# Blocks 0 and 1 by seven products too, and weights split into high and low parts in every unit

## The chip, the cores and the metric

One Trainium2 chip, one of its cores. The metric is the device time of one execution in microseconds (us). TensorE (PE) multiplies, VectorE (DVE), ScalarE (ACT) and GpSimd (POOL) do the rest, and SyncE (SP) issues the transfers between the chip's memory (HBM) and the on-chip SBUF. Each engine works through its own list in order; semaphores join the lists.

## The reference, cut to what matters

```
hn   = rms_norm(x, norm_g)                          # x: 4096 + 32 rows of 1024
proj = hn @ w_in                                    # 1024 x 3584
h, b, c, z, a, g, zb = split(proj)                  # seven sections of 512
out_a  = b * causal_conv3(c * h) * silu(z)
conv_b = causal_conv31(a * sigmoid(g)) + conv_b_bias
out_b  = silu(layer_norm(conv_b)) * silu(zb)
y = rms_norm(x + concat(out_a, out_b) @ w_out, final_norm_g)
```

The histories of the two convolutions are outputs too.

## The kernel before, in words

The tokens are 9 blocks of 460 (12 of padding). Every float32 product is made of three matmuls: each operand is split into a high part and a low part (operand minus high part), and `split_product` adds high x high (L1737), high x low (L1738) and low x high (L1739). A matmul of 128 x 128 weights on 460 tokens is the unit of work here.

The first projection runs in **5 units**: unit 0 has blocks 0 and 1, units 1 to 3 two blocks each, unit 4 block 8. A unit has **14 periods**, in the order of `ORDER` (ga0 zz0 hc0 ga1 bz0 hc1 bz1 ga2 zz1 hc2 ga3 bz2 hc3 bz3), each for 128 columns of each of two sections: ga makes v (for conv31), hc makes u = c h (for conv3), bz the gate of group A, zz the two silu gates. Period n is 14 x unit + position, 0 to 69; periods 13, 27 and 41 are the last of units 0, 1 and 2.

- **Unit 0** has four `standing_tile`s a period, 24 matmuls each, 96 in all. The weights of the period come as float32 and are split there: high parts on ScalarE (`weight_high`, L1132), low parts on VectorE (`weights_low`, L1396, 128x1024 twice), the four sums of weights that the products of later units need on GpSimd (`weight_sums`, L929 to L934, and their low parts, L940). All eight finished chunks, high and low, go to HBM (`weight_forms`).
- **Units 1 to 3** multiply by the method of Strassen: seven products of 12 matmuls, 84 a period, in the order P1, P5, P6, P2, P7, P3, P4 (`strassen_product`). P3 waits for ScalarE's copy of P5, P6 for that of P1, P7 for that of P6, P4 for that of P7 (`copy`, L1172). P1 starts when the last tile of two periods ago is read. Each product reads a finished chunk of weights from a ring of 9 slots (`load_form`), and a *form* of x: a sum or difference of quarters of the unit's scaled x, split into high and low. The seven forms of the next unit are made around its start: sums on VectorE (`form_sum`, L1405 to L1417), high parts on ScalarE (`form_high`, L1150), low parts on VectorE (`form_low`, L1424).
- **Unit 4** multiplies plainly: two tiles of two half tiles of 12 matmuls a period (`late_tile`), each with a finished chunk of the ring.

Beside these: VectorE makes the 620 taps of conv31 (L1554), a number for each period (`tap_quota`: 10 in an inner period of units 0 to 3, 12 in unit 4); in `finish(n-1)`, run in period n, it multiplies the first block of a section (L1479 for u) and runs conv3 (`conv_a`, L1503, L1506). In units 1 to 3 `first_tile_sums` (L1439, L1442) adds products for the first block, GpSimd adds the last quarter (`last_quarter`, L1002) and makes the second block of v, u and the gate (`second_block`, L976, L980, L984), and ScalarE applies the gates in place (`gate_in_place`, L1183). GpSimd also scales x (`x_scale`, L905). In unit 4 the layer norm of group B begins: GpSimd's `sums` (L1012, L1015) and `sum_low` (L1020) wait for conv_b to come back from HBM, TensorE makes the mean and the variance (`channel_mean`, L1844), and the out projection's weights are split (`out_weight_low`, L1032). After unit 4 come layer norm, out projection and the last norm for all tokens; the change doesn't touch that part.

The order on each engine is written out by hand, as one loop over the periods for each; the taps are placed by `tap_plan`. `sets` are the four quarters of the two last periods, `ps` is PSUM, `w_ring` the ring, `xf` the forms of x, `x_raw` the scaled x.

## Time and profile before

| what | value |
|---|---|
| median of 3 runs | 1589.77 us (1589.3 to 1589.8) |
| the profiled execution | 1589.94 us, its span 1588.1 us |
| instructions: TensorE / VectorE / ScalarE / GpSimd | 7196 / 1196 / 721 / 434 |
| first matmul on x | 24.03 us |
| HBM read / written | 277.70 MB / 101.18 MB |

Span is from the first to the last instruction on record. The trace gives for every instruction its start, its length and, in brackets, how long its engine stood idle before it and what it waited for. Matmul records overlap, so their number in a stretch tells more than their lengths. The matmul lengths on record are those of a pipeline and aren't to be multiplied by a count; the time from one to the next is.

### The profile page before, as it was taken

Reading aid. Unit: us, or ns where it says so; the run is one execution under the profiler, and the core shown is the slowest. Engines: PE = TensorE matmul, PEld = TensorE weight load, DVE = VectorE, ACT = ScalarE, POOL = GpSimd, SP = SyncE. Lnnn points to the kernel's source line nnn. Section 1 sums busy time; section 2 is a strip of 40 time slices with the busy share of each in tenths; the row PEclk is TensorE's granted clock in tenths of the full one; section 3 lists DMA queues with packets and bytes.
Section 4 is the critical chain, followed back from the end, with each engine's and each line's share of the span. In section 5 each row is a group of like instructions: output and inputs, shape, how many; then the busy total and the mean of one; then the engine's idle time right before and its main releaser. Section 6 shows DMA issues by size and latency. Waiting matters only on the chain.

```text
span 1588.1 us, 19038 instructions
## 1 busy us (share of the span) xinstructions
PE 1544.5 (97%) x7196; PEld 1356.8 (85%) x7196; DVE 1281.0 (81%) x1196; ACT 509.0 (32%) x721; POOL 501.1 (32%) x434
## 2 busy tenths in 40 slices
PE   4899999999999999999999999999999999999998
PEld 4789999988888888888888888888887888888886
DVE  5699899997877998879798878785997777777752
ACT  4443433333333243332253312232231232323221
POOL 3756869201232221132221131113220333332310
PEclk9999999999999999999999999999999999999999
DMA  4898889689987788897779877779576443545441
GB/s 157 321 332 311 324 305 353 241 296 304 283 285 241 232 254 295 277 290 252 234 222 310 259 231 243 220 256 318 192 241 198 138 145 142 184 160 182 142 142 63
DMA packets 105613, 380.06 MB, mean 239 GB/s; under 512 B 16228, under 2 KB 20196, under 8 KB 101944
## 3 DMA queue, kind: packets, MB, share of 16 engines
q1 hardware_dynamic: 105528, 378.93, 71.4%
q8 instruction: 54, 0.88, 0.2%
q14 instruction: 31, 0.25, 0.0%
HBM read 277.70 MB, written 101.18 MB: 239 GB/s over the span
## 4 chain that ended last, share of the span: by engine, by line
PE 90%; DVE 6%; issue 2%; DMA 1%; POOL 1%; ACT 0%; POOLq 0%; DVEq 0%; SPq 0%; ACTq 0%
PE ps L1737 30%; PE ps L1739 30%; PE ps L1738 30%; DVE ps L1554 3%; DVE xf L1396 1%; DVE xf L1388 1%; DVE x_raw L1382 1%; DMA conv_b<-conv_spill 1%; DMA w_ring<-weight_forms 0%; PE ps L1844 0%; DVE w_ring L1396 0%; PE ps L1845 0%; POOL ln_tmp_a_f L1012 0%; POOL w_out_split L1032 0%; DVE conv_b L1571 0%
## 5 line engine op out<-in xcount | busy, mean ns | idle before, releaser
L1554 DVE SCALAR_TENSOR_TENSOR ps<-v,conv_b_taps,ps 128x920 f32<-128x920 f32 (+2 forms) x580 | 630.9, 1088 | 18.0
L1737 PE MATMUL ps<-xf,w_ring 128*128 128x460 f32 x1624 | 605.2, 373 | 3.3 <-DMA w_ring<-weight_forms 2.1
L1739 PE MATMUL ps<-xf,w_ring 128*128 128x460 f32 x1624 | 604.1, 372 | 0.0
L1738 PE MATMUL ps<-xf,w_ring 128*128 128x460 f32 x1624 | 602.7, 371 | 0.0
L1737 PEld LDWEIGHTS ps<-xf,w_ring 128*128 128x128 f32 x1624 | 306.4, 189 | 39.0 <-issue 3.3
L1738 PEld LDWEIGHTS ps<-xf,w_ring 128*128 128x128 f32 x1624 | 306.4, 189 | 34.7
L1739 PEld LDWEIGHTS ps<-xf,w_ring 128*128 128x128 f32 x1624 | 305.9, 188 | 35.1
L1172 ACT ACTIVATE sets<-ps 128x460 f32<-128x460 f32 x168 | 92.8, 552 | 460.3 <-PE ps L1739 456.5
L1737 PE MATMUL ps<-w_out_split,mixed 128*128 128x512 f32 x528 | 206.5, 391 | 0.0
L1739 PE MATMUL ps<-w_out_split,mixed 128*128 128x512 f32 x528 | 206.4, 391 | 0.0
L1738 PE MATMUL ps<-w_out_split,mixed 128*128 128x512 f32 x528 | 206.3, 391 | 0.0
L1002 POOL TENSOR_TENSOR sets<-sets 128x460 f32<-128x460 f32 x42 | 55.0, 1310 | 425.1 <-ACT sets L1172 425.1
L1737 PEld LDWEIGHTS ps<-w_out_split,mixed 128*128 128x128 f32 x528 | 99.5, 189 | 21.8 <-issue 1.0
L1739 PEld LDWEIGHTS ps<-w_out_split,mixed 128*128 128x128 f32 x528 | 99.5, 188 | 20.9
L1738 PEld LDWEIGHTS ps<-w_out_split,mixed 128*128 128x128 f32 x528 | 99.4, 188 | 20.8
L1342 ACT ACTIVATE ps<-h_rows 128x1024 f32<-128x1024 f32 (+1 forms) x33 | 34.0, 1029 | 213.6 <-DVE h_rows L1685 213.6
L879 POOL TENSOR_TENSOR row_mean_sq_eps<-row_mean_sq,rms_eps 128x1 f32<-128x1 f32 (+1 forms) x33 | 9.0, 274 | 282.2 <-ACT ps L1342 282.2
L1737 PE MATMUL ps<-xf 128*128 128x460 f32 x224 | 84.7, 378 | 10.8 <-DVE xf L1388 10.8
L1739 PE MATMUL ps<-xf 128*128 128x460 f32 x224 | 84.3, 376 | 0.0
L1738 PE MATMUL ps<-xf 128*128 128x460 f32 x224 | 83.6, 373 | 0.0
L905 POOL TENSOR_TENSOR x_raw<-x_raw,rstd_spread 128x460 f32<-128x460 f32 x56 | 69.4, 1272 | 44.9 <-DMA rstd_spread<-rstd_spill 44.9
L1685 DVE TENSOR_TENSOR h_rows<-ps,x_rows_again 128x1024 f32<-128x1024 f32 (+1 forms) x33 | 40.2, 1218 | 39.3 <-PE ps L1739 39.3
(144 smaller groups left out, 1575.0 us busy)
## 6 DMA issues: line engine op xcount, KB each, us to landing
w_ring<-weight_forms SPq DMA_DIRECT2D x350, 512.0 KB, 5.1
weight_forms<-xf SPq DMA_DIRECT2D x14, 2048.0 KB, 11.2
weight_forms<-w_ring SPq DMA_DIRECT2D x14, 2048.0 KB, 13.5
x_raw<-in_xT SPq DMA_DIRECT2D x18, 920.0 KB, 11.4
x_rows_again<-in_x_prompt SPq DMA_DIRECT2D x32, 512.0 KB, 4.3
out_y_prompt<-h_rows SPq DMA_DIRECT2D x32, 512.0 KB, 3.0
xf_f<-in_w_in SPq DMA_DIRECT2D x26, 512.0 KB, 6.3
x_row<-in_x_prompt SPq DMA_DIRECT2D x28, 460.0 KB
```

Of the source, the lines that this page charges most:

```text
L905: pool.tensor_tensor(part, part, spread[:, 0:TB], ALU.mult).then_inc(x_scaled, 1)
L1002: pool.tensor_tensor(sets[:, s, QC, :], sets[:, s, QC, :], sets[:, s, QD, :], ALU.add).then_inc(c22_made, 1)
L1172: act.activation(sets[:, n % 2, quarter, :], ps[:, bank, 0:TB], ACT.Copy).then_inc(copied, 1)
L1342: act.activation(out_pair(2)[0:rows, :], hrow[0:rows, s, :], ACT.Square, scale=RMS_SCALE, accum_out=ssq[0:rows, s:s + 1]).then_inc(h_sumsq, 1)
L1382: dve.scalar_tensor_tensor(part, part, gain[:, k:k + 1], ps[:, FIRST_BANK[b], 0:TB], ALU.mult, ALU.mult).then_inc(x01_scaled, 1)
L1388: dve.tensor_tensor(standing_x(b, 1, 2 * r, 2 * r + 2), st[:, 2 * b + r // 2, 2 * (r % 2):2 * (r % 2) + 2, :], standing_x(b, 0, 2 * r, 2 * ...
L1396: dve.tensor_tensor(chunks(g, 2 * f, 2 * f + 2)[:, :, 1, :], raw_weights(g, f), chunks(g, 2 * f, 2 * f + 2)[:, :, 0, :].bitcast(F32), ALU. ...
L1554: dve.scalar_tensor_tensor(dst, window, wb[:, j, k:k + 1], part, ALU.mult, ALU.add).then_inc(taps_done, 1)
L1685: dve.tensor_tensor(hrow[0:rows, s, :], out_pair(s)[0:rows, :], raw[0:rows, s, :], ALU.add).then_inc(h_done, 1)
L1737: pe.matmul(out, ahi, bhi, start=(start and x == 0), stop=False, skip_group_check=goes_on)
L1738: pe.matmul(out, ahi, blo, start=False, stop=False, skip_group_check=goes_on)
L1739: mm = pe.matmul(out, alo, bhi, start=False, stop=(stop and x == len(terms) - 1), skip_group_check=goes_on)
```

## The change

- Unit 0 goes through the seven products too. Its `standing_tile` is gone, and `first_tile_sums`, `last_quarter` and `second_block` run there as in units 1 to 3. Periods 0 and 1 are interleaved (`FIRST_PRODUCTS`), and seven forms of x are made at the start from halves (`first_sum_of_x`, `first_form_high`, `first_form_low`).
- The order of products is P1, P5, P6, **P3**, P7, **P2**, P4.
- Only the four sums of weights are stored (`weight_sums`, 2 MB a period for 4 MB). The weights as they stand are read again as float32 (`load_chunk`, 256 KB for the 512 KB of a finished chunk) and split again: in units 1 to 3 three chunks a period, high on ScalarE (`ring_high`), low on GpSimd (`ring_low`); in unit 4 all 56 (`late_high`, `late_low`), 128x512 each.
- In unit 0 ScalarE, VectorE and GpSimd handle chunks of 128x512 one at a time: three low parts of weights on VectorE, four sums and four low parts on GpSimd.
- At a unit's start the forms of P3 and P2 change places, and P4's form gets a place of its own.
- Taps per inner period are 9, 10, 11, 11 and 12 in units 0 to 4. The first layer norm's steps on VectorE move from positions 8, 10 and 12 to 9, 11 and 13, and the variance from 8 to 9.

```diff
-CHUNK_OF = [0, 4, 5, 1, 6, 7, 3]
-P1, P5, P6, P2, P7, P3, P4 = range(7)
+P1, P5, P6, P3, P7, P2, P4 = range(7)
+
+WEIGHT_OF = {P1: 0, P2: 1, P4: 3}
+SUM_OF = {P5: 0, P6: 1, P3: 2, P7: 3}
+S1, S2, S4, S3 = range(4)
+SUM_ORDER = [S1, S2, S4, S3]
+PRODUCT_OF_SUM = [P5, P6, P3, P7]
+PRODUCT_OF_WEIGHT = [P1, P2, P4]
...
+FIRST_PRODUCTS = [(0, P1), (1, P1), (0, P2), (1, P2), (0, P5), (0, P3), (0, P6), (0, P7), (0, P4),
+                  (1, P5), (1, P6), (1, P3), (1, P7), (1, P4)]
...
-    return 10 if u < 4 else 12
+    return [9, 10, 11, 11, 12][u]
...
-        forms_d = nc.dram_tensor("weight_forms", [G14, P, 8 * 2 * HC], F32).ap()
+        forms_d = nc.dram_tensor("weight_sums", [G14, P, 4 * 2 * HC], F32).ap()
...
+                if i in WEIGHT_OF:
+                    load_chunk(g, WEIGHT_OF[i], slot)
+                else:
+                    src = forms_d[g].rearrange("p (c l m) -> p c l m", c=4, l=2)
+                    sp.dma_start(ring[:, slot, :, :].bitcast(F32), src[:, SUM_OF[i]]).then_inc(ring_in[slot], 16)
...
-                load_ring(r // 4, r % 4, late_slot(r))
+                load_chunk(r // 4, r % 4, late_slot(r))
...
+            def sums_of_weights(g):
+                for x in SUM_ORDER:
+                    weight_sum(g, x)
+                for x in SUM_ORDER:
+                    sum_low_half(g, x)
+
+            def ring_low(n, i):
+                pool.wait_ge(ring_hi, weights_split(n, i))
+                w = weights(n, i)
+                pool.tensor_tensor(w[:, 1, :], weights(n, i, True)[:, 1, :], w[:, 0, :].bitcast(F32),
+                                   ALU.subtract).then_inc(ring_lo, 1)
...
+            def rings_low(n):
+                if n >= G14:
+                    ring_low(n, P2)
+                    ring_low(n, P4)
+                if G14 <= n + 1 < III:
+                    ring_low(n + 1, P1)
...
+            for n in range(1, III):
+                last_quarter(n - 1)
                 edges(n - 1)
-                if n + 1 < II:
-                    weight_sums(n + 1)
-                    sums_low(n + 1)
-                carry(n - 1)
+                if n < G14 - 1:
+                    second_block(n - 1)
+                    carry(n - 1)
+                    sums_of_weights(n + 1)
+                else:
+                    rings_low(n)
+                    second_block(n - 1)
+                    carry(n - 1)
...
 
             for n in range(III, PERIODS):
                 g = n - III
                 if n == III:
                     last_quarter(n - 1)
                 edges(n - 1)
+                late_low(4 * g + 2)
+                late_low(4 * g + 3)
                 second_block(n - 1)
                 carry(n - 1)
+                if 1 <= g <= KC:
+                    out_weight_low(g - 1)
+                late_low(4 * g + 4)
+                late_low(4 * g + 5)
                 if g == 3:
                     sums(0, 0)
                     sum_low(0)
...
+                    wait_a_free(act, n)
+                    copy(n, P1, QA, copied_a)
                 if ends and w < 4:
                     form_high(w, P1)
                 elif ends:
                     x8_high(0)
                     x8_high(1)
+                rings_high(n)
                 gate_in_place(n - 1)
-                if begins:
-                    form_high(unit(n), P3)
                 wait_d_free(act, n)
                 copy(n, P5, QD, copied_d)
+                if begins:
+                    form_high(unit(n), P4)
                 if ends and w == 4:
                     x8_high(2)
                     x8_high(3)
...
-            first_ln = {5: centre, 6: square_sums, 7: var_low, 8: normalise, 10: gate, 12: b_low}
+            first_ln = {5: centre, 6: square_sums, 7: var_low, 9: normalise, 11: gate, 13: b_low}
...
+
+            for n in range(1, III):
                 w, g = unit(n) + 1, n % G14
+                if n == 1:
+                    weight_low(1, P4)
+                elif n < G14:
+                    weight_low(n, P2)
+                    weight_low(n, P4)
                 if g == 0:
-                    form_low(unit(n), P2)
-                if n > II:
-                    first_tile_sums(n - 1)
+                    form_low(unit(n), P3)
+                first_tile_sums(n - 1)
                 if g == 0:
+                    form_sum(unit(n), 3)
                     finish(n - 1)
                     form_low(unit(n), P7)
-                    form_sum(unit(n), 3)
-                    form_low(unit(n), P3)
+                    form_low(unit(n), P2)
                     form_low(unit(n), P4)
...
-            for n, t in TILE_AT:
-                standing_tile(n, t)
-                if (n, t) == (0, 1):
+            for n, i in FIRST_PRODUCTS:
+                strassen_product(n, i)
+                if (n, i) == (0, P1):
                     first_statistics(1)
-                if (n, t) == (1, 0):
                     first_rstd(1)
```

**ScalarE, the last period of unit 1 (period 27).** From the copy of P1 on; `sets<-ps` are copies of products, `xf<-` the high parts of the next unit's forms. Before:

```order
L1172 ACTIVATE sets<-ps 128x460 [waits product_done,spilled_ab_1]
L1150 ACTIVATE xf<-x_raw 128x920 [waits x_scaled,product_done]
L1150 ACTIVATE xf<-x_raw 128x920
L1172 ACTIVATE sets<-ps 128x460 [waits product_done,spilled_dc_1,last_quarter_summed]
L1172 ACTIVATE sets<-ps 128x460 [waits product_done,spilled_ab_1]
L1150 ACTIVATE xf<-xf_f 128x920 [waits x_form_sums,product_done]
L1150 ACTIVATE xf<-xf_f 128x920
```

After (L1250 copies, L1224 makes high parts):

```order
L1250 ACTIVATE sets<-ps 128x460 [waits product_done,spilled_ab_1]
L1224 ACTIVATE xf<-x_raw 128x920 [waits x_scaled,product_done]
L1224 ACTIVATE xf<-x_raw 128x920
L1188 ACTIVATE w_ring<-w_ring_f 128x512 [waits w_ring_in_1]
L1188 ACTIVATE w_ring<-w_ring_f 128x512 [waits w_ring_in_2]
L1188 ACTIVATE w_ring<-w_ring_f 128x512 [waits w_ring_in_3]
L1250 ACTIVATE sets<-ps 128x460 [waits product_done,spilled_dc_1,last_quarter_summed]
L1250 ACTIVATE sets<-ps 128x460 [waits product_done,spilled_ab_1]
L1224 ACTIVATE xf<-xf_f 128x920 [waits x_form_sums,product_done]
```

Three high parts of weights, each behind its load, have moved in between the first form of x and the copy of P5.

**GpSimd, periods 27 and 28.** `u<-sets` is u's second block, `conv_a_acc<-` the gate's second block, `sets<-sets` a last quarter. Before:

```order
L966 COPY u<-u_carry 128x2 [waits made_by_pool,made_by_vector]
L980 TENSOR_TENSOR u<-sets 128x460 [waits first_tile_summed,last_quarter_summed]
L996 COPY u_carry<-u 128x2 [waits made_by_pool]
L1002 TENSOR_TENSOR sets<-sets 128x460 [waits copied_c,copied_d]
L984 TENSOR_TENSOR conv_a_acc<-conv_a_acc,sets 128x460 [waits made_by_vector,last_quarter_summed]
```

After:

```order
L998 COPY u<-u_carry 128x2 [waits made_by_pool,made_by_vector]
L959 TENSOR_TENSOR w_ring<-w_ring_f,w_ring 128x512 [waits w_ring_hi] x3
L1014 TENSOR_TENSOR u<-sets 128x460 [waits first_tile_summed,last_quarter_summed]
L1030 COPY u_carry<-u 128x2 [waits made_by_pool]
L1036 TENSOR_TENSOR sets<-sets 128x460 [waits copied_c,copied_d]
L959 TENSOR_TENSOR w_ring<-w_ring_f,w_ring 128x512 [waits w_ring_hi] x3
L1018 TENSOR_TENSOR conv_a_acc<-conv_a_acc,sets 128x460 [waits made_by_vector,last_quarter_summed]
```

Three low parts of weights stand ahead of each second block.

**GpSimd, unit 4, from its fourth period on (position 3).** `ln_tmp_a_f<-conv_b` is the first of the layer norm's sums, `w_out_split` a low part of the out projection's weights. Before:

```order
L966 COPY u<-u_carry 128x2 [waits made_by_pool,made_by_vector]
L1012 TENSOR_TENSOR ln_tmp_a_f<-conv_b 128x1024 [waits first_conv_b_in_0]
L1015 TENSOR_TENSOR ln_tmp_a_f<-ln_tmp_a_f 128x512 [waits ln_sums]
L1020 TENSOR_TENSOR ln_tmp_a<-ln_tmp_a_f,ln_tmp_a 128x512 [waits ln_sum_hi]
L1032 TENSOR_TENSOR w_out_split<-w_out_split_f,w_out_split 128x1024 [waits w_out_hi]
```

After:

```order
L998 COPY u<-u_carry 128x2 [waits made_by_pool,made_by_vector]
L974 TENSOR_TENSOR w_ring<-w_ring_f,w_ring 128x512 [waits w_late_hi] x2
L1066 TENSOR_TENSOR w_out_split<-w_out_split_f,w_out_split 128x1024 [waits w_out_hi]
L974 TENSOR_TENSOR w_ring<-w_ring_f,w_ring 128x512 [waits w_late_hi] x2
L1046 TENSOR_TENSOR ln_tmp_a_f<-conv_b 128x1024 [waits first_conv_b_in_0]
L1049 TENSOR_TENSOR ln_tmp_a_f<-ln_tmp_a_f 128x512 [waits ln_sums]
L1054 TENSOR_TENSOR ln_tmp_a<-ln_tmp_a_f,ln_tmp_a 128x512 [waits ln_sum_hi]
```

The low parts of chunks (L974) stand ahead of the sum, and the next ones behind it.

## Rows read from the trace of the kernel before

**Rows 1.** The page: busy time and share of each engine; the chain by engine.
```profile
PE 1544.5 (97%) x7196; PEld 1356.8 (85%) x7196; DVE 1281.0 (81%) x1196; ACT 509.0 (32%) x721; POOL 501.1 (32%) x434
...
PE 90%; DVE 6%; issue 2%; DMA 1%; POOL 1%; ACT 0%; POOLq 0%; DVEq 0%; SPq 0%; ACTq 0%
```

**Rows 2.** Stretches: length, busy PE PEld DVE ACT POOL (x instructions), PEclk, DMA, GB/s.
```profile
24.03:74.90 50.87, 45.92 (x208) 40.23 (x209) 34.02 (x31) 23.23 (x26) 38.22 (x21) 1.00 0.63 228
316.40:561.60 245.20, 245.20 (x1173) 220.26 (x1172) 204.32 (x191) 81.89 (x132) 55.89 (x62) 1.00 0.85 271
1054.70:1230.00 175.30, 164.72 (x750) 144.78 (x749) 142.01 (x191) 43.89 (x51) 36.57 (x25) 0.96 0.75 243
1145.00:1146.00 1.00, 1.00 (x4) 0.85 (x4) 0.93 (x3) 0.00 (x0) 0.96 (x2) 0.50 1.05 414
```

**Rows 3.** Time line of the head: start, length, engine, line, shapes [idle before].
```profile
17.94 4.92 DVE L1382 SCALAR_TENSOR_TENSOR x_raw<-x_raw,gain,ps 128x460 f32<-128x460 f32 x8 [3.38 <-issue]
...
22.78 2.13 DVE L1388 TENSOR_TENSOR xf<-x_raw,xf 128x920 fp32r<-128x920 f32 x2
...
24.03 0.72 PE L1737 MATMUL ps<-xf 128*128 128x460 f32 x1 [6.19 <-DVE xf L1388]
```

**Rows 4.** Groups in unit 0, VectorE and GpSimd: busy, mean ns | idle before.
```profile
L1554 DVE SCALAR_TENSOR_TENSOR ps<-v,conv_b_taps,ps 128x938 f32<-128x938 f32 x114 | 136.7, 1199 | 3.7
...
L1396 DVE TENSOR_TENSOR w_ring<-xf_f,w_ring 128x1024 fp32r<-128x1024 f32 x12 | 24.1, 2032 | 9.2 <-ACT w_ring L1132 9.1
...
L1506 DVE SCALAR_TENSOR_TENSOR conv_a_acc<-u,conv_a_taps,conv_a_acc 128x910 f32<-128x910 f32 x8 | 12.3, 1532 | 0.3
...
L940 POOL TENSOR_TENSOR w_ring<-w_ring_f,w_ring 128x1024 fp32r<-128x1024 f32 x12 | 34.8, 2921 | 1.6 <-ACT w_ring L1132 1.2
...
L905 POOL TENSOR_TENSOR x_raw<-x_raw,rstd_spread 128x460 f32<-128x460 f32 x16 | 20.1, 1290 | 1.4 <-DMA rstd_spread<-rstd_spill 1.4
...
L929 POOL TENSOR_TENSOR w_ring_f<-xf_f 128x512 f32<-128x512 f32 x6 | 9.1, 1523 | 29.3 <-DMA xf_f<-in_w_in 29.3
...
L934 POOL TENSOR_TENSOR w_ring_f<-xf_f,w_ring_f 128x512 f32<-128x512 f32 x6 | 8.0, 1340 | 0.5
```

**Rows 5.** Time line of ScalarE after a ga and after a zz period.
```profile
462.39 0.53 ACT L1172 ACTIVATE sets<-ps 128x460 f32<-128x460 f32 x1
464.58 0.56 ACT L1172 ACTIVATE sets<-ps 128x460 f32<-128x460 f32 x1 [1.66 <-PE ps L1739]
...
480.88 0.54 ACT L1172 ACTIVATE sets<-ps 128x460 f32<-128x460 f32 x1
482.16 0.56 ACT L1172 ACTIVATE sets<-ps 128x460 f32<-128x460 f32 x1 [0.73 <-PE ps L1739]
```

**Rows 6.** Time line of VectorE, ScalarE and GpSimd about period 27.
```profile
544.98 0.64 DVE L1479 TENSOR_TENSOR u<-ps,sets 128x460 f32<-128x460 f32 x1 [1.55 <-PE ps L1739]
...
549.90 2.08 DVE L1405 TENSOR_TENSOR xf_f<-x_raw 128x1840 f32<-128x1840 f32 x1 [1.12 <-PE ps L1739]
...
568.92 2.07 DVE L1424 TENSOR_TENSOR xf<-x_raw,xf 128x1840 fp32r<-128x1840 f32 x1
...
552.93 1.83 ACT L1150 ACTIVATE xf<-xf_f 128x920 fp32r<-128x920 f32 x2
...
557.51 0.56 ACT L1172 ACTIVATE sets<-ps 128x460 f32<-128x460 f32 x1 [0.76 <-PE ps L1739]
...
543.57 1.18 POOL L980 TENSOR_TENSOR u<-sets 128x460 f32<-128x460 f32 x1 [1.64 <-DVE sets L1442]
...
561.16 2.90 POOL L984 TENSOR_TENSOR conv_a_acc<-conv_a_acc,sets 128x460 f32<-128x460 f32 x1
```

**Rows 7.** Time line of TensorE and GpSimd in unit 4.
```profile
1143.33 0.79 PE L1844 MATMUL ps<-ln_tmp_b,mean_w 128*128 128x512 f32 x1 [3.61 <-DVE ln_tmp_b L1582]
...
1101.42 2.40 POOL L1012 TENSOR_TENSOR ln_tmp_a_f<-conv_b 128x1024 f32<-128x1024 f32 x1 [21.89 <-DMA conv_b<-conv_spill]
...
1105.93 1.27 POOL L1020 TENSOR_TENSOR ln_tmp_a<-ln_tmp_a_f,ln_tmp_a 128x512 fp32r<-128x512 f32 x1 [0.74 <-ACT ln_tmp_a L1216]
```

686 lines of the change are left out of this document (352 added, 334 removed).

## The prediction

> **What bounds the kernel now.** I read the page's busy shares and its chain first: TensorE is busy for 97% of the span and carries 90% of the chain [rows 1], so a matmul removed is time removed, as long as nothing else comes late. Then the stretches: from 316.40 to 561.60 us TensorE is busy for the whole 245.20 us, while VectorE is busy for 204.32 us and GpSimd for 55.89 us; in the first two periods, up to 74.90 us, TensorE is busy for 45.92 of 50.87 us [rows 2]. A copy of ScalarE that waits for TensorE starts at 464.58 us, the same copy of the next period at 482.16 us [rows 5]: a period is 17.58 us, and one of its 84 matmuls 0.209 us. I call T the start of a period's product P1, so its seven products end at T+2.5, 5.0, 7.5, 10.0, 12.6, 15.1 and 17.6. Everything below asks which of them is late.
>
> **1. Matmuls removed.** 14 periods with 7 products of 12 in place of 4 tiles of 24: 168 fewer. 168 x 0.209 = **-35.1 us**.
>
> **2. The start.** Before, the first matmul runs at 24.03 us, after eight scalings (4.92 us) and a low half of 1.06 [rows 3]. After, P1 needs half a block, but VectorE first makes the sums for the second block too; I put the scaling at 18.6 us and the first low half at 22.2. Then the seven forms of x are made in a row on VectorE: 8 more scalings (4.9 us), 8 half sums and 14 low halves at about 1.06, with ScalarE's high halves between. By these durations P3(0) starts at 44.4, P6(0) at 50.3 and P7(0) at 54.5 us, each when VectorE has made its form; P4(1) at 71.8 us waits for ScalarE, which stands in front of a row load. Periods 0 and 1 end at about 74.3 us against 74.90 [rows 2], though they have 24 matmuls (5.0 us) fewer. Part 1 has counted these 5.0 us, so the start gives back 5.0 - 0.6 = **+4.4 us** (0 to +10).
>
> **3. Periods 2 to 12.** VectorE has per period 9 taps of 1.20 us, three low halves of weights (about 1.0, half of the 2.03 us of a row twice as long), two tile sums of 0.64 [rows 6], and the end of the last section, 0.64 us or, with three convolution steps of up to 1.53, about 4.3 [rows 4]: 15 to 20 us, mean near 17.5, against 17.6. GpSimd has 4 sums of weights at 1.34 to 1.52 us, 4 low halves at 1.46 (half of 2.92) and two 128x460 at 1.2, about 14 us, and in four periods four scalings of 1.29 more: over 19 us [rows 4]. Both are near full, and ScalarE's copy of P5, which P3 waits for, stands behind gates that wait for VectorE. I followed it period by period: 2 us at period 2 (VectorE comes some 4 us late out of the start), 1 us each at 4 and 8, and 4 at 9, since the first tap of a new job waits for v's second block, late on GpSimd. **+8 us** (0 to +22, the upper end if the four full GpSimd periods each lose the 2 us that they are over and VectorE's long ones as much).
>
> **4. Inner periods of units 1 to 3.** ScalarE has three chunks of weights more (0.53 each, as a copy of about the same size) between the copy of P1 and the copy of P5. In a ga period that copy ended at 462.92 and P6 at 464.58, when the next copy starts: 1.66 us of room for 1.6 us of work. After a zz period it ended at 481.42 and P6 at 482.16, 0.74 of room, so 0.9 us lost, six times: **+5 us** (0 to +10) [rows 5].
>
> **5. The last period of a unit and the first of the next.** Here I expect the largest loss. Before, in period 27 (T = 544.95, VectorE's wait for TensorE ends there): u is whole at T-0.2 (GpSimd, 543.57 + 1.18), the first sum of forms starts at 549.90 = T+5.0, ScalarE splits two forms from 552.93 and copies P7 at 557.51 = T+12.6, the moment P7 ends [rows 6]. No room is left there. After, ScalarE has the high half of P1's form (1.83 us) and three weight chunks ahead, done at T+6.5; GpSimd makes the chunks' low halves first (1.27 us each [rows 7]), and only then u's second block: T+10.6. VectorE's u1 doesn't wait for it, its first convolution step does; the convolution ends at T+13.7, and with a form low that is queued between, the first sum of forms at T+15.7. ScalarE, in order, waits for it before the copy of P7: 15.7 + 3.7 + 0.6 = T+20.0. P4, which needs that copy, wants to start at T+15.1: **5 us** lost. In the next period VectorE has in a row a form's low half, the tile sums, a fourth sum, z, and P7's low half. z waits for b's second block, again behind three low halves of weights, which ScalarE's three splits of forms, its copy of P1 and its own part of the weights put off to about T+28.3; b's block is there at T+34 to 36, z at 37, P7's low half at 39 (T still that of period 27). P7 wants to start at 17.6 + 5.0 + 10.0 = 32.6: **6 us** lost. Before, P7's low half started at 568.92 and ended 1.6 us before it was wanted [rows 6]. Periods 27/28 and 41/42: 2 x 11 = **+22 us** (10 to 30). At 13/14 the first load of the ring is released by VectorE's low halves of period 13 itself, and ScalarE waits for it before the copy of P5. Later than wanted by 1.4 (load), 3.7 (one sum and split of a form), 3.9 (three low halves on GpSimd) and 5.2 (the next period's share): **+14 us** (6 to 20).
>
> **6. Unit 4.** Weights are split by ScalarE and GpSimd, 56 chunks, each wanted 2.5 us after the last. GpSimd stood idle for 21.89 us until 1101.42 us for conv_b [rows 7]; before, nothing was queued behind its sum that TensorE wanted soon. After, the low halves of chunks 18 and on are. T of period 56 is 1054.7, chunk 18 is wanted at 1054.7 + 45.1 = 1099.8, and comes at 1101.4 + 2.4 (sum) + 1.3 + 1.3 + 0.2 + 1.3, about 1107: 7 us lost. After that four slots hold three half tiles (7.5 us) of lead for load, high and low half, and three long GpSimd instructions and the second set of sums can break it: 11 us at most likely. Against them, TensorE stood idle for 10.58 us between 1054.70 and 1230.00, with a mean clock of 0.96 [rows 2], 3.61 us of it in one wait at 1143.33 [rows 7]; 4% of 175 us is 7 us, so 17 us lie there, and I take 14 to be swallowed by the new waits. **+4 us** (-5 to +14).
>
> **7. The clock.** Two us after the 3.61 us wait TensorE was granted 0.50 of its clock, 1.2 GHz, in the us from 1145.00; over the 175.3 us from 1054.70 the mean is 0.96, so 7 us of full clock were missing behind all waits there [rows 2, 7]. I take 2.3 us for a wait of this size, an estimate, and add it once for each of the three units' ends: **+7 us** (0 to +15).
>
> **Sum.** -35.1 + 4.4 + 8 + 5 + 22 + 14 + 4 + 7 = +29 us. The profiled run took 1589.94 us, its span 1588.1, the median of three is 1589.77: 1590 + 29 = **1619 us**.
>
> **A rule weighed.** GpSimd's 128x460 sum took 1.18 us at 543.57 and 2.90 us at 561.16 [rows 6], and VectorE was adding SBUF to SBUF beside the second and not beside the first. The Trainium skill ("SBUF — State Buffer", section "SBUF: two separate sides") says that the two engines share a port pair as an exclusive lock, held for a whole instruction, also where VectorE has two inputs in SBUF. By this rule each GpSimd low half of part 5 may wait out a form of 2.07 us; the trace agrees in kind. It is the page's name for rival C.
>
> **Rivals.**
> A, faster: GpSimd makes u's and b's second block early enough and ScalarE isn't late. It decides at period 27: if the first sum of forms ends before T+11, the copy of P7 is in time and parts 4, 5 and 7 are near nothing. For it: GpSimd was busy for 56 of 245 us [rows 2]. Against it: the order puts the low halves first, and these wait for ScalarE. -35.1 + 4.4 + 8 + 4 = -19: 1571 us.
> B, no change: only the first loss of each pair (2 x 5), 13/14 at its lower end of 6, no loss of clock: -35.1 + 4.4 + 8 + 5 + 10 + 6 + 4 = +2: 1592 us.
> C, slower still: GpSimd and VectorE hold each other up. Where VectorE makes forms, three low halves take 2.9 us in place of 1.27, 5 us more at each of three units' ends; and in unit 0 GpSimd's eight weight instructions take 1.8 in place of 1.4, 3 us in each of its four full periods. 15 + 12 = +27 on the forecast: 1646 us. It decides where a GpSimd instruction of 128x512 is over 2 us.
> That the products aren't saved is no rival: TensorE's list is shorter by 168 matmuls.
>
> **How the numbers follow.** Forecast (1600 to 1635) 0.62, A 0.17, C 0.15, B 0.06. The ends of the terms' ranges won't fall together; 1574 to 1643 takes in the forecast and B, and leaves out about half of A, half of C. A measurement can tell 0.2%, 3.2 us: faster 0.18 (A and the low edge of B), same 0.05 (the rest of B), slower 0.77 (forecast and C).
>
> **What would show it.** TensorE's waits should stand at the units' ends, name VectorE's form lows and ScalarE's copies, and add up to 10 us or more at each; the first sum of forms of period 27 should start 13 to 16 us after T; the second period should end near 74 us; one wait of 5 to 9 us should stand near chunk 18. I am wrong if TensorE is unbroken across period 28, or if periods 2 to 13 take under 215 us (12 x 17.6 = 211) or over 245.

## The result

The changed kernel takes **1677.83 us** (median of 4, 1676.47 to 1681.56) against 1589.53 us (1588.59 to 1589.80): **5.6% slower**, ratio 1.056, 95% interval 1.0542 to 1.0579. The forecast was 1619 us, range 1574 to 1643. The direction was right, the size is three times the forecast's, 88 us in place of 29, and outside the range.

The page of the changed kernel, busy time and chain:

```profile
PE 1549.1 (92%) x7028; PEld 1343.7 (80%) x7028; DVE 1314.5 (78%) x1240; ACT 629.8 (38%) x999; POOL 775.5 (46%) x670
...
PE 62%; DVE 9%; ACT 8%; issue 8%; DMA 7%; POOL 6%; SPq 1%; POOLq 0%; ACTq 0%; DVEq 0%
```

TensorE was busy for 97% of a span of 1588.1 us [rows 1]; now for 92% of 1676.5. It carries 62% of the chain in place of 90%. GpSimd went from 501 to 776 us of work, ScalarE from 509 to 630, VectorE from 1281 to 1315. TensorE's waits, in total, with their number and the longest:

```profile
PE ps L1833 <- ACT sets L1250: 52.5, 24, 7.3
PE ps L1833 <- POOL w_ring L974: 21.8, 3, 10.5
PE ps L1833 <- issue: 14.5, 3, 5.0
...
PE ps L1833 <- DVE xf L1494: 12.4, 4, 5.0
```

The copies of products (L1250) are the largest by far; L974 is GpSimd's low part of a chunk in unit 4. Stretches, columns as in [rows 2]: start, periods 2 to 12, periods 15 to 26, unit 4.

```profile
24.03:88.66 64.63, 48.45 (x183) 40.81 (x182) 53.05 (x51) 27.27 (x41) 34.13 (x27) 0.82 0.30 106
88.66:314.60 225.94, 202.93 (x926) 178.43 (x925) 186.67 (x181) 100.00 (x175) 168.18 (x143) 0.95 0.58 204
366.90:582.70 215.80, 213.43 (x1009) 188.80 (x1009) 173.41 (x166) 83.56 (x146) 98.03 (x92) 1.00 0.72 222
1130.80:1301.20 170.40, 148.57 (x677) 131.78 (x675) 147.59 (x182) 68.07 (x99) 110.74 (x80) 0.92 0.46 144
```

All 5376 matmuls of the first projection are on record in both traces (5544 before), so the start of each product can be counted off. This gives where the time went; "before" is less the 12 matmuls (2.51 us) saved in each period of unit 0:

| stretch | before, less the matmuls saved | after | lost | forecast |
|---|---|---|---|---|
| up to period 2 | 69.9 | 88.7 | +18.8 | +4.4 |
| periods 2 to 12 | 193.7 | 225.9 | +32.3 | +8 |
| periods 13 and 14 | 35.0 | 52.4 | +17.3 | +14, clock +2.3 |
| 27 and 28; 41 and 42 | 71.0 | 99.6 | +28.6 | +22, clock +4.7 |
| the other 36 of units 1 to 3 | 632.9 | 646.7 | +13.8 | +5 |
| unit 4 | 153.9 | 170.4 | +16.5 | +4 |
| behind it | 379.1 | 375.3 | -3.8 | 0 |

Period 55 takes 17.6 us in both.

With the matmuls, -35.1, that is +88.4 us, the difference of the spans.

The steps from one matmul to the next split each loss in two. In periods 2 to 12 TensorE's waits (steps over 0.55 us) lose 24.4 us, and steps that are merely longer than 0.209 us lose 8.1 us, beside a mean granted clock of 0.95. At the three ends (13/14, 27/28, 41/42) it is 33.9 us of waits and 12.7 us of slow steps, 0.7 us of which the kernel before has as well.

**The units' ends** came as forecast, nearly instruction by instruction. Period 27 now starts at T = 582.70. Rows of GpSimd, VectorE, ScalarE, TensorE:

```profile
592.11 1.17 POOL L1014 TENSOR_TENSOR u<-sets 128x460 f32<-128x460 f32 x1
...
593.37 0.70 DVE L1595 TENSOR_SCALAR conv_a_acc<-u,conv_a_taps 128x920 f32<-128x920 f32 x1 [9.71 <-POOL u L1014]
...
596.41 2.07 DVE L1508 TENSOR_TENSOR xf_f<-x_raw 128x1840 f32<-128x1840 f32 x1
...
602.03 0.53 ACT L1250 ACTIVATE sets<-ps 128x460 f32<-128x460 f32 x1
...
602.61 0.47 PE L1833 MATMUL ps<-xf,w_ring 128*128 128x460 f32 x1 [4.69 <-ACT sets L1250]
...
622.52 0.72 PE L1833 MATMUL ps<-xf,w_ring 128*128 128x460 f32 x1 [4.97 <-issue]
```

u's second block runs at T+9.4 and ends at T+10.6, VectorE's convolution starts behind it, and the first sum of forms at 596.41 = T+13.7 in place of T+5.0 [rows 6]. ScalarE copies P7 at T+19.3 (T+20.0 forecast). TensorE loses 4.69 us there and 4.97 us in period 28. Behind each wait the granted clock is at its lower level, 1.2 GHz: 0.50 from 603.6 to 605.6 us and from 622.5 to 626.5 us. From 618.0 to 622.5, while TensorE does nothing, the mean is 0.76, so it falls within that wait.

**Unit 0** has the largest miss. By period, 2 to 12 lose 2.6, 4.9, 1.1, 4.8, 10.1, 4.4, 2.4, 0.0, 0.0, 1.0 and 1.4 us. The worst, period 6, ends at 200 us. ScalarE, the transfer of the row of x from the chain of waits, and TensorE:

```profile
183.43 0.64 ACT L1179 ACTIVATE w_ring<-w_ring_f 128x512 fp32r<-128x512 f32 x1 [2.36 <-DMA w_ring_f<-in_w_in]
192.47 1.06 ACT L1153 ACTIVATE x_row<-x_row 115x1024 f32<-115x1024 f32 x1 [8.41 <-DMA x_row<-in_x_prompt]
...
179.55 12.90 DMA x_row<-in_x_prompt
...
195.25 0.75 PE L1833 MATMUL ps<-xf,w_ring 128*128 128x460 f32 x1 [7.31 <-ACT sets L1250]
```

ScalarE stood for 8.41 us for this row, in front of the copy of P7; SyncE had issued it 12.90 us before it landed. SyncE itself:

```profile
176.29 0.28 SPq L604 DMA_DIRECT2D rstd_spill<-x_rstd_columns  x1
...
177.03 1.35 SPq L635 DMA_DIRECT2D w_ring_f<-in_w_in  x2
...
179.55 0.40 SPq L590 DMA_DIRECT2D x_row<-in_x_prompt  x1
```

From 161 us on it had waited for a reciprocal root (L604, `send_rstd`) that GpSimd makes behind its eight weight instructions; then came a store of 1 MB, two loads of weights, a second store, and the row behind all of them.

The kernel before had the same root in the same queue, ahead of its loads of weights, and one place for raw weights from period 2 on, too. What it had twice is the place of the finished chunks: those of even periods and those of odd ones. Now each product of unit 0 has one slot, refilled only when the same product of the period before is done and, for a sum, its store has landed. And TensorE now multiplies by the sums in unit 0, where it used the plain weights alone. The last low parts that period 7 needs, before on VectorE, after on GpSimd:

```profile
164.37 5.57 DVE L1396 TENSOR_TENSOR w_ring<-xf_f,w_ring 128x1024 fp32r<-128x1024 f32 x2
```

```profile
195.79 5.46 POOL L947 TENSOR_TENSOR w_ring<-w_ring_f,w_ring 128x512 fp32r<-128x512 f32 x4 [3.04 <-ACT w_ring L1184]
```

Period 7 started at 176.1 us before, 6.2 us after their end; now it starts at 200.0 us, 1.3 us ahead of it. No run here gives the finished chunks their second place back.

### The profile page after: what moved, and what is told of

Its sections match the earlier page's. It is cut to its first block, busy times and chain, and to the rows that moved or that the text cites. A ratio compares the mean times of both kernels' runs of the same rounds, so it can differ in the third digit from the quotient of the medians.

```text
span 1676.5 us, 19454 instructions
## 1 busy us (share of the span) xinstructions
PE 1549.1 (92%) x7028; PEld 1343.7 (80%) x7028; DVE 1314.5 (78%) x1240; ACT 629.8 (38%) x999; POOL 775.5 (46%) x670
## 4 chain that ended last, share of the span: by engine, by line
PE 62%; DVE 9%; ACT 8%; issue 8%; DMA 7%; POOL 6%; SPq 1%; POOLq 0%; ACTq 0%; DVEq 0%
PE ps L1833 21%; PE ps L1835 20%; PE ps L1834 20%; DMA x_row<-in_x_prompt 4%; DVE ps L1644 3%; ACT w_ring L1188 2%; POOL w_ring L947 2%; ACT sets L1250 2%; ACT sets L1261 1%; POOL w_ring_f L939 1%; DVE xf L1527 1%; DMA w_ring_f<-in_w_in 1%; ACT L1261 1%; DMA sets<-in_w_in 1%; DVE w_ring L1500 1%
## 5 line engine op out<-in xcount | busy, mean ns | idle before, releaser
L1833 PE MATMUL ps<-xf,w_ring 128*128 128x460 f32 x1784 | 682.7, 383 | 103.8 <-ACT sets L1250 52.5
L1835 PE MATMUL ps<-xf,w_ring 128*128 128x460 f32 x1784 | 674.2, 378 | 0.0
L1834 PE MATMUL ps<-xf,w_ring 128*128 128x460 f32 x1784 | 673.3, 377 | 0.0
L1644 DVE SCALAR_TENSOR_TENSOR ps<-v,conv_b_taps,ps 128x920 f32<-128x920 f32 (+2 forms) x580 | 630.6, 1087 | 17.6
L1833 PEld LDWEIGHTS ps<-xf,w_ring 128*128 128x128 f32 x1784 | 344.6, 193 | 164.0 <-ACT sets L1250 73.9
L1834 PEld LDWEIGHTS ps<-xf,w_ring 128*128 128x128 f32 x1784 | 344.6, 193 | 38.8
L1835 PEld LDWEIGHTS ps<-xf,w_ring 128*128 128x128 f32 x1784 | 343.4, 192 | 40.3
L1250 ACT ACTIVATE sets<-ps 128x460 f32<-128x460 f32 x224 | 122.0, 549 | 466.3 <-PE ps L1835 454.0
L959 POOL TENSOR_TENSOR w_ring<-w_ring_f,w_ring 128x512 fp32r<-128x512 f32 x126 | 169.2, 1373 | 269.3 <-ACT w_ring L1188 269.3
L1036 POOL TENSOR_TENSOR sets<-sets 128x460 f32<-128x460 f32 x56 | 72.9, 1301 | 184.5 <-ACT sets L1250 184.4
L974 POOL TENSOR_TENSOR w_ring<-w_ring_f,w_ring 128x512 fp32r<-128x512 f32 x56 | 77.1, 1394 | 53.6 <-ACT w_ring L1202 53.3
L939 POOL TENSOR_TENSOR w_ring_f<-w_ring_f 128x512 f32<-128x512 f32 x52 | 73.4, 1419 | 52.3 <-DMA w_ring_f<-in_w_in 29.0
L947 POOL TENSOR_TENSOR w_ring<-w_ring_f,w_ring 128x512 fp32r<-128x512 f32 x56 | 80.8, 1474 | 27.2 <-ACT w_ring L1184 25.9
L912 POOL TENSOR_TENSOR x_raw<-x_raw,rstd_spread 128x460 f32<-128x460 f32 x56 | 75.5, 1379 | 5.5 <-DMA rstd_spread<-rstd_spill 5.5
```

The costliest lines, as they stand in the source:

```text
L912: pool.tensor_tensor(part, part, spread[:, 0:TB], ALU.mult).then_inc(x_scaled, 1)
L939: pool.tensor_tensor(to[x], a, b, op).then_inc(w_sum, 1)
L947: pool.tensor_tensor(w[:, 1, :], weights(g, PRODUCT_OF_SUM[x], True)[:, 1, :], w[:, 0, :].bitcast(F32), ALU.subtract).then_inc(w_lo_s, 1)
L959: pool.tensor_tensor(w[:, 1, :], weights(n, i, True)[:, 1, :], w[:, 0, :].bitcast(F32), ALU.subtract).then_inc(ring_lo, 1)
L974: pool.tensor_tensor(ring[:, slot, 1, :], ring_f32[:, slot, 1, :], ring[:, slot, 0, :].bitcast(F32), ALU.subtract).then_inc(late_lo, 1)
L1036: pool.tensor_tensor(sets[:, s, QC, :], sets[:, s, QC, :], sets[:, s, QD, :], ALU.add).then_inc(c22_made, 1)
```

## The experiments

Every stretch below is counted off from TensorE's products. Times are medians of two runs beside the kernel before on the same chip (1590 to 1592 us). A stretch comes from one trace each, and kernels with the same instructions in unit 0 show how far it repeats: periods 2 to 12 take 224.6 to 226.0 us in the changed kernel, e3, e4, e5, e6 and e10, 232.0 and 230.8 in e7 and e8, 222.9 and 226.1 in e9 and e11. A difference of 3 us in this stretch is therefore not clear.

### Is it the row of x?

```diff
             for n in range(1, G14):
+                if n <= 8:
+                    load_row(1, n - 1)        # SyncE: out of prepare_x
                 if n + 1 < G14:
                     load_tile(n + 1, 0)
```

> Change against the changed kernel: in periods 1 to 8 of unit 0 SyncE issues the load of the next row of x ahead of the period's weight loads and of the store of sums, not behind them. Nothing is left out. Theory R (the row comes late): in the changed kernel ScalarE stood before the copy of P7 for this row (8.42 us until 82.94, 5.89 us until 103.42, 8.41 us until 192.47), and P4 waited for that copy by 6.1, 2.3, 3.5, 3.4, 7.3, 2.6 and 2.1 us. With the row early these waits and the slow stretches behind them go: period 13 starts at 285 to 292 us in place of 314.6, the whole takes about 1650 us (1645 to 1660). Rival S (VectorE and GpSimd are full in unit 0, as the forecast had it): TensorE waits for other copies in their place, period 13 starts after 305 us, the whole is within 8 us of 1678.

```diff
-                squares_of_rows(n)
-                gains(n)
                 wait_c_free(act, n)
                 copy(n, P7, QC, copied_c)
+                squares_of_rows(n)
+                gains(n)
```

> Change against the changed kernel: in all periods to 55 ScalarE copies P7 before it squares the row of x and multiplies by the gains, not after. SyncE's order stays. Nothing is left out. Theory R: P4 no longer waits, but the row is as late as before and ScalarE still stands before it, now with the next sums of weights behind it, which GpSimd and the next period's P5 want; so a part of the 32 us of unit 0 comes back: period 13 starts at 290 to 303 us, the whole takes 1655 to 1668 us. Rival S: no gain, 1675 to 1682 us.

Measured: 1677.1 and 1676.0 us, against 1677.8 (e2's move holds for all units). The start got 5 to 6 us shorter (period 2 begins at 83.4 and 82.6 in place of 88.7), but periods 2 to 12 took 228.6 and 228.5 us in place of 225.9. **Theory R fell.** In e2 ScalarE still waits 33.2 us in all for rows, now behind the copy, and TensorE waits for GpSimd's low parts in its place (12.2 us). In e1 the wait for the row is gone, and ScalarE stands in nearly the same place for something else:

```profile
159.92 0.63 ACT L1181 ACTIVATE w_ring<-w_ring_f 128x512 fp32r<-128x512 f32 x1 [6.31 <-DMA w_ring_f<-in_w_in]
...
186.08 0.63 ACT L1181 ACTIVATE w_ring<-w_ring_f 128x512 fp32r<-128x512 f32 x1 [11.91 <-DMA w_ring_f<-in_w_in]
```

Here it is the float32 weights of the next period (`weight_high(n+1, P1)`), 6.31 and 11.91 us. And period 9, which lost nothing in the changed kernel, now loses 6.3 us in e1 and 6.6 in e2.

### The chain of loads, then VectorE

```diff
# ScalarE, unit 0
+                    copy(n, P7, QC, copied_c)
                     weight_high(n + 1, P1)
+                    for x in SUM_ORDER:
+                        sum_high_half(n + 1, x)
...
                 squares_of_rows(n)
                 gains(n)
# SyncE: e1's move, the first row ahead of store_sums(0, 0), and
                     load_tile(n + 1, 1)
+                prepare_x(n - 1, False)       # send_rstd, out of period n-1
```

> Changes against the changed kernel, all in unit 0, nothing left out. SyncE: the row of x is loaded ahead of the weights, the first one ahead of the first stores, and the send of the reciprocal root stands behind the next period's weight loads. ScalarE: the copy of P7 directly behind that of P6, then the next P1 weights and the sums' high parts, then the row and the gains. The two runs before this one, each with one of these moves, moved unit 0 by 3 us only, since ScalarE then stood in the same place for a chunk of weights (6.31 and 11.91 us) that SyncE issued late: in period 5 SyncE itself stood for the root, from 161 to 176.3 us. Theory Q (SyncE's one queue makes the loads late, and whatever ScalarE waits for stands before the copy of P7): with all three moved, periods 2 to 12 take 195 to 207 us in place of 225.9, and the whole 1645 to 1660 us. Rival (GpSimd is full in unit 0, and the single place for raw weights ties load, sums and splits into one chain of over 17.6 us a period): 215 us or more for periods 2 to 12, TensorE then waits at P5 and P6 for GpSimd's low parts.

Measured: 1675.2 us; periods 2 to 12 took 232.0 us, more than before. Theory Q fell too. But this kernel shows a ring that could set such a pace. ScalarE's split of P2's and P4's weights, SyncE's loads, GpSimd's sums:

```profile
194.34 1.14 ACT L1183 ACTIVATE w_ring<-w_ring_f 128x512 fp32r<-128x512 f32 x2
...
215.24 1.14 ACT L1183 ACTIVATE w_ring<-w_ring_f 128x512 fp32r<-128x512 f32 x2
...
195.97 1.96 SPq L635 DMA_DIRECT2D w_ring_f<-in_w_in  x2
...
207.20 5.30 POOL L943 TENSOR_TENSOR w_ring_f<-w_ring_f 128x512 f32<-128x512 f32 x4 [2.93 <-DMA w_ring_f<-in_w_in]
```

From 194.34 to 215.24 are 20.9 us: splits, low parts on VectorE, the load (issued at 196 to 198, landed at 207.2), four sums, ScalarE's high parts, row and gains, and the next split. There is one place for raw weights (`raw_tile`), and all of it has to go round in a period: 17.6 us where nothing is late, 20.1 us in the kernel before. That everything comes round once in 20.9 us is so whatever sets the pace; whether the ring does has to be tested. The next kernel takes the stores and the row out of that ring:

```diff
 # SyncE
                     load_tile(n + 1, 1)
+                prepare_x(n - 1, False)
+                store_sums(n, 0)
                 store_sums(n, 1)
...
-                    store_sums(n + 1, 0)
 # ScalarE, unit 0: copy P6, row, gains, copy P7, weight_high(n + 1, P1), sums
```

> Changes against the changed kernel, all in unit 0, nothing left out. As e7, but SyncE issues the period's two weight loads before either store of sums and before nothing else but the row; ScalarE: copy P6, row, gains, copy P7, then the next period's P1 weights and the sums' high parts. Theory Z (unit 0 runs at the pace of a ring through the one place for raw weights): in e7 ScalarE split P2's and P4's weights at 194.34 and again at 215.24, 20.9 us apart, and between stood VectorE's low parts (to 197.6), the load (issued 196 to 198, landed 207.2, behind a store of 1 MB and the row), GpSimd's four sums (5.3 us), ScalarE's high parts, row and gains. With the store and the row out of it the ring takes 16 to 18 us, so periods 2 to 12 take 195 to 207 us in place of 225.9 and the whole 1645 to 1660 us. Rival: another order makes another thing late (the slots of the sums are free only when stored), and it stays at 220 us or more.

Measured: 1669.7 us, periods 2 to 12 222.9 us: 9.1 less than in e7, but only 3.0 us less than in the changed kernel, which is not clear, of the 20 or more expected. Now TensorE waits for the copy of P5 (6.3 us once) and for GpSimd's low parts, and ScalarE's gates for VectorE's tile sums (26.3 us in eight waits). The next three decide between these:

```diff
# e12, VectorE
                 w = ACC_W[uu]
+                if uu == 0 and 0 < k < KB - 1:
+                    w = TB
# e13, SyncE; ScalarE and GpSimd wait for period 1's weights only
             def load_tile(g, f):
+                if g >= 2:
+                    return
```

> Change against e9 (222.9 us for periods 2 to 12): the middle 29 of the 31 taps of each of unit 0's four jobs run over 460 columns in place of 938. It leaves out the rest of these taps. A tap should take 0.71 in place of 1.20 us, so VectorE has some 4 us less in each period of unit 0. Theory V (VectorE's list sets the pace of unit 0, since ScalarE's gates and the copy of P5 wait for its tile sums): periods 2 to 12 take 198 to 208 us. Theory Z (the ring through the one place for raw weights, load included): 218 us or more.

> Change against e9: in unit 0 the weights of periods 2 to 13 are not loaded and nothing waits for them; the weights of period 1 are split and summed in their place. It leaves out those loads, so the products are not the reference's. It frees GpSimd's sums and ScalarE's high parts of the wait for a load and takes 12 MB of transfers away. Theory Z: periods 2 to 12 take 195 to 207 us in place of 222.9. Theory V: VectorE is as full as before, 215 us or more.

> Both, e12's short taps and e13's missing loads, against e9; it leaves out both parts. If each theory holds for a part of unit 0's loss and one hides the other, this gives more than the sum of the two alone: periods 2 to 12 near 194 us, 11 periods of 17.6. If it stays over 205 us, GpSimd's eight weight instructions a period (11 us and more) or ScalarE's order hold a third part.

| kernel | whole | periods 2 to 12 | against e9 |
|---|---|---|---|
| e9 | 1669.7 | 222.9 | |
| e12, taps halved | 1658.6 | 211.0 | -11.9 |
| e13, no loads | 1672.6 | 227.4 | +4.5 |
| e14, both | 1644.2 | 199.9 | -23.0 |

One stretch of e9, e12 and e14 (84 to 306 us; columns as above):

```profile
84.00:306.00 222.00, 201.64 (x921) 175.59 (x920) 190.89 (x190) 101.15 (x177) 169.16 (x145) 0.97 0.57 207
```

```profile
84.00:306.00 222.00, 207.12 (x959) 181.24 (x958) 161.82 (x199) 107.95 (x187) 180.33 (x155) 0.98 0.59 214
```

```profile
84.00:306.00 222.00, 212.13 (x1000) 188.54 (x1000) 166.17 (x206) 109.84 (x190) 180.59 (x155) 0.99 0.46 171
```

VectorE is busy for 191 of 222 us in e9 and for 162 in e12. **VectorE's list is the first limit that the runs find**: with its taps halved 11.9 us go, without the loads nothing. (That e13 takes 4.5 us more is little over what the stretch repeats to, and unexplained.) The loads are the second, right behind: they show only with the taps short, where they are worth another 11.1 us. With both gone 6.5 us remain to 193.4 (11 x 17.58), 2.6 us of them in period 2 and 3.4 in period 9. So theory V gave 11.9 of the 15 to 25 us that it expected (211.0 against 198 to 208), theory Z by itself nothing. The order of SyncE's and ScalarE's lists, the row and the root among them, gave nothing clear by itself (e1, e2, e7, e9); that these two limits hid its worth is possible and not shown.

### The units' ends

```diff
                 else:
-                    rings_low(n)
                     second_block(n - 1)
                     carry(n - 1)
+                    rings_low(n)
```

> Change against the changed kernel: from period 13 on GpSimd makes the second block of u, v or the gate before the three low parts of weights, not after. Nothing is left out. Theory (the forecast's part 5): at the units' ends u's second block (at 592.11, T+9.4 in period 27) and the gate's (618.04) come some 8 us earlier, the first sum of forms of period 27 starts at T+5 to T+7 in place of T+13.7, the 4.7 us wait for the copy of P7 and the 5.0 us one of the next period go, with the slow clock behind each: 27/28 and 41/42 lose under 3 us each in place of 14, and 13/14 some 5 us less than its 17: about 1650 us (1645 to 1660). Rival: the low parts of weights, now later, make TensorE wait for them (P2, P4, the next P1), or VectorE's chain of forms is late by itself: 1670 us or more.

Measured: 1654.3 us, 23.5 less. Period 27 takes 17.6 us in place of 24.1, 41 takes 18.5 in place of 24.7: the theory holds for the first loss of each pair. Not for the second: period 28 takes 23.5 and 42 even 27.8 us. GpSimd's low parts and b's block, and VectorE's forms, in period 27:

```profile
582.66 8.97 POOL L959 TENSOR_TENSOR w_ring<-w_ring_f,w_ring 128x512 fp32r<-128x512 f32 x3 [5.01 <-ACT w_ring L1188]
...
594.69 2.90 POOL L1018 TENSOR_TENSOR conv_a_acc<-conv_a_acc,sets 128x460 f32<-128x460 f32 x1
...
582.24 2.08 DVE L1508 TENSOR_TENSOR xf_f<-x_raw 128x1840 f32<-128x1840 f32 x1 [1.12 <-PE ps L1835]
584.23 3.16 DVE L1527 TENSOR_TENSOR xf<-x_raw,xf 128x1840 fp32r<-128x1840 f32 x1
587.32 3.16 DVE L1513 TENSOR_TENSOR x_raw<-x_raw 128x1840 f32<-128x1840 f32 x1
```

VectorE's sum takes 2.08 us at 582.24, begun while GpSimd was idle; the next two take 3.16 each. GpSimd's three low parts take 8.97 us, 2.99 each in place of 1.27 [rows 7]. **They take turns**: a pair, one of each, has 2.07 + 1.27 = 3.34 us of work by the lone times, and one goes by every 3.1 to 3.2 us (584.23 to 587.32 to 590.51). The Trainium skill ("SBUF — State Buffer", "SBUF: two separate sides") calls it an exclusive lock, no split of bandwidth; the trace agrees, also in the number. The next run's pair doesn't take full turns, 2.4 us for 3.5 us of lone work, and there the measurement decides.

> Change against e3: in units 1 to 3 GpSimd writes the place of a chunk's low part with zero times its high part, an instruction that reads one 128x512 tile from SBUF, in place of the subtraction that reads two. It leaves out the low parts of the weights as they stand in units 1 to 3. In e3 GpSimd's three low parts at period 27 took 8.97 us (2.99 each) and VectorE's sums and low parts of forms beside them 3.1 in place of 2.07 us, and period 28 took 23.5 us. Theory P (the two engines hold each other up where both read SBUF): GpSimd's instruction takes 0.7 to 1.3 us, VectorE's are mostly back at 2.07, period 28 takes 17.6 to 20 us, and 41/42 lose some 8 us less: about 1640 us. Rival (it is ScalarE's order and the length of VectorE's list): VectorE's forms stay at 3 us or period 28 stays over 22 us, 1650 us or more.

```diff
-                pool.tensor_tensor(w[:, 1, :], weights(n, i, True)[:, 1, :], w[:, 0, :].bitcast(F32), ALU.subtract)
+                pool.tensor_scalar(w[:, 1, :], w[:, 0, :].bitcast(F32), 0.0, None, ALU.mult)
```

```profile
583.69 7.80 POOL L958 TENSOR_SCALAR w_ring<-w_ring 128x512 fp32r<-128x512 f32 x3 [5.16 <-ACT w_ring L1186]
...
585.25 2.48 DVE L1525 TENSOR_TENSOR xf<-x_raw,xf 128x1840 fp32r<-128x1840 f32 x1
...
806.54 4.41 POOL L958 TENSOR_SCALAR w_ring<-w_ring 128x512 fp32r<-128x512 f32 x3
```

Measured: 1649.2 us, 5 less than e3, whose own two runs are 5.8 us apart. In an inner period, at 806.54, the new instruction takes 1.47 us, longer than the subtraction's 1.27, so as a relief of GpSimd it was a poor choice. Beside VectorE it takes 2.6 us, and VectorE's forms take 2.48 in place of 3.16 us: a pair has 2.07 + 1.47 = 3.54 us of lone work and goes by every 2.4 us (585.25 to 587.65). With one input of GpSimd's from SBUF in place of two, the engines overlap in part. Period 28 takes 22.4 us, 41 and 42 together 40.7 in place of 46.3. It lies between the two expectations: shorter forms go with part of the second loss, and the rest stands with them at 2.4 us. How much is the turn-taking's and how much that of ScalarE's and VectorE's lists, this run does not settle.

### Splitting on the fly, priced whole

```diff
# units 1 to 4: a stored sum in the place of each split chunk
-                if i in WEIGHT_OF:
-                    load_chunk(g, WEIGHT_OF[i], slot)
-                else:
...
             def rings_low(n):
+                return
             def rings_high(n):
+                return
```

> Change against the changed kernel: in units 1 to 4 every chunk of weights is loaded high and low, 512 KB, and none is split by ScalarE and GpSimd. It leaves out the splitting of the weights as they stand in units 1 to 4, and multiplies by stored sums in their place. It prices the splitting on the fly. Theory (splitting costs what stands from period 14 on: 14 us at each of two ends, 13.8 us in inner periods, 16.5 us in unit 4, some of 13/14's 17): the whole takes 1678 - 28 - 14 - 12 - 7 = about 1617 us (1605 to 1630), and period 13 starts at 314 us as before, since unit 0 has none of it. Rival: the losses at the units' ends come from the new order of forms and products and stay: over 1640 us.

Measured: 1624.4 us, so splitting on the fly, less what the larger loads cost, is worth 53.5 us. Period 13 starts at 314.5 us, as in the changed kernel (314.6). Periods 27/28 take 35.9 (35.5 before), 41/42 38.5, the inner periods lose 1.5 us in place of 13.8, unit 4 takes 155.9 us in place of 170.4. 13/14 keep most of their loss: 45.1 us, 10.0 over the 35.0 of the kernel before. There TensorE waits 3.6 us for the copy of P7, ScalarE in front of it 6.4 us for VectorE's first sum of forms, and VectorE has no gap over 0.9 us: its list alone is too long there.

### ScalarE's order in inner periods

```diff
-                rings_high(n)
                 gate_in_place(n - 1)
                 wait_d_free(act, n)
                 copy(n, P5, QD, copied_d)
+                rings_high(n)
```

> Change against the changed kernel: from period 13 on ScalarE applies the gates and copies P5 first and splits the three chunks of weights behind that, not before. Nothing is left out. Theory (the forecast's part 4): the wait of P3 for the copy of P5, 1.1 us after each zz period of units 1 to 3 and 3.9 us at period 13, goes, and so does the 0.3 us that most other inner periods have lost: 13.8 + 4 us at most, so 1660 to 1667 us. Rival: the chunks, split later, make P2 or P4 wait (GpSimd's low part comes behind), and the loss only changes its place: 1673 us or more.

Measured: 1692.1 us, 14 more. In most inner periods the loss is gone, as expected (17.6 us), but 35, 37, 40, 49, 51 and 54 now take 19.4 to 22.2 us, and all three unit ends grow. In period 37 and the one before it, ScalarE's gate and VectorE:

```profile
784.24 1.13 ACT L1261 ACTIVATE sets<-sets 128x460 f32<-128x460 f32 x2 [3.59 <-DVE sets L1542]
...
770.27 1.24 DVE L1641 TENSOR_SCALAR ps<-v,conv_b_taps,conv_b_bias_sb 128x920 f32<-128x920 f32 x1 [5.87 <-POOL v L1009]
771.54 12.13 DVE L1644 SCALAR_TENSOR_TENSOR ps<-v,conv_b_taps,ps 128x920 f32<-128x920 f32 x10
783.58 0.63 DVE L1542 TENSOR_TENSOR sets<-ps,sets 128x460 f32<-128x460 f32 x1
```

The gate waits for VectorE's tile sums, these stand behind taps, and the first tap of the job had stood 5.87 us for v's second block (L1009). GpSimd makes that block behind the three low parts, and these now wait for ScalarE's later splits. Four of the six periods (37, 40, 51, 54) are the second behind a ga period; 35 and 49 are ga periods themselves, and in 35 the gate waits 4.3 us for the tile sums as well. With e3's order of GpSimd the same edit has none of this (e8, below: all 36 at 17.6 us).

### Unit 4

The three long waits of TensorE in unit 4, and what ended late before each: ScalarE's gate, GpSimd's first sum, SyncE's store of u's state:

```profile
1142.95 0.72 PE L1833 MATMUL ps<-xf,w_ring 128*128 128x460 f32 x1 [6.95 <-POOL w_ring L974]
...
1189.12 0.72 PE L1833 MATMUL ps<-xf,w_ring 128*128 128x460 f32 x1 [4.41 <-POOL w_ring L974]
...
1273.13 0.72 PE L1833 MATMUL ps<-xf,w_ring 128*128 128x460 f32 x1 [10.47 <-POOL w_ring L974]
...
1139.81 1.13 ACT L1261 ACTIVATE sets<-sets 128x460 f32<-128x460 f32 x2 [12.15 <-DVE sets L1542]
...
1181.86 2.40 POOL L1046 TENSOR_TENSOR ln_tmp_a_f<-conv_b 128x1024 f32<-128x1024 f32 x1 [3.44 <-DMA conv_b<-conv_spill]
...
1264.02 0.34 SPq L701 DMA_DIRECT2D out_new_a_prompt<-u  x1
```

```diff
# SyncE: load_late ahead of store_convs and spill (spill one place later)
# ScalarE, GpSimd: chunks 2 and 3 ahead of gate_in_place / last_quarter
-                if g == 3:
+                if g == 4:
                     sums(0, 0)
                     sum_low(0)
```

> Changes against the changed kernel, all in unit 4: SyncE issues the loads of chunks ahead of the stores of conv31, spills and states; chunks 2 and 3 are split ahead of the last gates; the first sums of the layer norm stand one position later on GpSimd and ScalarE. Nothing is left out. Theory (each of the three long waits, 6.95, 4.41 and 10.47 us, comes from one instruction that waits for VectorE or conv_b in front of a chunk): periods 56, 60 and 67 take 10.0, 10 to 13 and 10 to 14 us in place of 18.6, 17.2 and 23.5: unit 4 is 20 to 29 us shorter, 1650 to 1658 us. Rival (GpSimd and ScalarE haven't the time for 56 chunks): the waits stand at other chunks, 1670 us or more.

Measured: 1680.1 us. Unit 4 takes 166.3 us in place of 170.4: 4 us of 20. Period 56 takes 14.9 for 18.6, 60 takes 15.8 for 17.2, 67 takes 16.4 for 23.5, but 57, 61 and 68 take 8.3 us more. The wait at the end of period 60 is now in front of the layer norm's mean, which needs the sums of conv_b, no longer in front of a chunk. And the time behind unit 4 grew from 375.3 to 380.8 us, which eats the rest. Mostly the rival: these waits move.

### Everything together

> All of the changes of e3, e5, e6 and e7 together, nothing left out. If the losses are independent: e3 gave 24 us, e5 should give 13, e6 20, e7 20: about 1600 us (1590 to 1620). If one place hides another (a later wait takes over at the units' ends, or VectorE's forms and GpSimd's low parts slow each other as they did in e3, 3.1 us for 2.07 and 3.0 for 1.27), it stays over 1620 us. Either way it tells whether the change can beat the kernel before, 1590.

> As e8 (everything of e3, e5 and e6), with e9's order in unit 0 in place of e7's. Nothing is left out. e8 took 1643 us. If theory Z holds, periods 2 to 12 are 25 us shorter than in e8 (230.8): 1612 to 1625 us. If it falls: 1640 us or more.

Measured: 1643.4 and 1643.1 us. The inner periods lose nothing (0.0 us of 13.8), 27 takes 17.6, unit 4 158.6. But in unit 0 periods 2 to 12 keep 230.8 and 226.1 us, and 42 takes 27.8 in e8 (27/28 and 41/42 together 90.0 in e11). What was gained in unit 4 is partly given back behind it: from its end on they take 382 us, the changed kernel 375; no run says why. It is 34 us better than the changed kernel and 3.2% slower than the kernel before; no version here beats that one.

## Why the prediction was wrong, point by point

- **Matmuls, -35.1**: right. Products of 2.51 us, inner periods of 17.58 where nothing is late.
- **Start, +4.4 (0 to 10), measured +18.8**: the order was right, the rest too short in three places. The forecast ran the forms in a row on VectorE, at their lone 1.06 us for 128x920. First, VectorE stood still for 4.04 us, for high parts that ScalarE makes behind a wait for TensorE's statistics; no term had this. Second, six of its steps that ran beside GpSimd took up to twice their lone time:

```profile
28.90 0.26 ACT L1147 ACTIVATE x_mean_square_eps<-ps,rms_eps 115x4 f32<-115x4 f32 x1 [6.23 <-PE ps L1844]
...
31.09 3.50 DVE L1494 TENSOR_TENSOR xf<-x_raw,xf 128x920 fp32r<-128x920 f32 x2 [4.04 <-ACT xf L1212]
...
37.64 4.29 DVE L1486 TENSOR_TENSOR xf_f<-x_raw 128x920 f32<-128x920 f32 x2
...
49.27 4.18 DVE L1486 TENSOR_TENSOR x_raw<-x_raw 128x920 f32<-128x920 f32 x4
...
34.67 6.29 POOL L947 TENSOR_TENSOR w_ring<-w_ring_f,w_ring 128x512 fp32r<-128x512 f32 x4 [1.05 <-DVE xf L1494]
```

  The two sums at 37.64 run beside the last of GpSimd's four low parts and go by at 2.15 us each; the four at 49.27 run alone, 1.05 each. P3(0) started at 48.5 for 44.4 forecast, P7(0) at 60.3 for 54.5. Third, P4(1) waits 6.1 us for the copy behind the row of x: named in the forecast, but with a row that lands at 70 us, not at 82.9. This is worth 5 to 6 us (e1, e2).
- **Periods 2 to 12, +8 (0 to 22), measured +32.3**: the step that failed. The work was forecast well: near 17.5 us a period on VectorE, where 17.0 were measured (186.67 us in 225.94). What failed is the price of lists that nearly fill the period, 8 us, got by following one period after the other with every load, store and root on time. The places were wrong too: 4 us at period 9 and 2 at period 2 were forecast, and the changed kernel lost 2.6 at period 2, nothing at 9, and 24 us in periods 3 and 5 to 7. In its place the runs show two limits behind one another: VectorE's list, 11.9 us with the taps halved (e12), and the loads into the one place for raw weights, another 11.1 us with the taps short (e14), of the 29.5 us that e9 loses. What e14 has left, 2.6 us at period 2 and 3.4 at period 9, is close to the forecast's 2 and 4. Single-buffered finished chunks, which the forecast did not weigh, would make each short lateness a wait of TensorE; this is read from the kernels, and no run tests it. Besides, the low parts of weights on VectorE took 1.38 us on average in place of 1.0, and 0.68 where GpSimd stood idle (at 16.84). The clock was counted at three places only; here slow steps make up 8.1 of the 32.3 us. The forecast's own sign of being wrong, periods 2 to 13 over 245 us, came true: 252.2.
- **Inner periods, +5 (0 to 10), measured +13.8**: the six periods behind a zz period were right, 1.2 us each for 0.9. The rest was put at zero by a margin of 1.66 - 1.6 us; nineteen of the others lose 0.3 us each. A margin of some hundredths is no margin.
- **The units' ends, +36 and clock +7, measured +45.9**: right in place and size; the waits come to 33.9 us, the clock to 12.7 in place of 7. At 27/28 and 41/42 the mechanism was right as well: e3 takes away the first loss, e4 most of both. At 13/14 it was right in part: of 17.3 us 10.0 stay in e4, where no weights are split on the way. Rival A's test (the first sum of forms ends before T+11) was the right one: it began at T+13.7 (596.41), and the copy of P7 was late.
- **Unit 4, +4 (-5 to 14), measured +16.5**: chunk 18 was right in place and size (period 60 loses 7.2 us, 4.41 of them waiting, for 7; the forecast's own terms add up to 1107.9 us, so to 8.1). Not foreseen were chunk 2 (ScalarE in front of gates that wait for VectorE's taps, 6.95 us) and chunk 46 (SyncE behind a store that waits for VectorE, 10.47 us).
- **Rivals**: C was given 0.15, and its time, 1646 us, is the nearest to the measured one, but its mechanism is not what made the difference. GpSimd's low halves were slow only in the second period of each pair:

```profile
610.97 7.11 POOL L959 TENSOR_TENSOR w_ring<-w_ring_f,w_ring 128x512 fp32r<-128x512 f32 x3 [5.37 <-ACT w_ring L1188]
```

  Three low halves take 7.11 us there and 3.8 us in period 27, against C's 2.9 each, and GpSimd's eight weight instructions in unit 0 took 1.45 us on average, near the forecast's 1.4 and not C's 1.8. All misses of the first projection have one sign: each step was sized with all other queues on time.

## What to carry to other kernels

When a change shortens the list of the busiest engine, work through the queues that only issue and wait as well: for each wait on SyncE write down what is queued behind it and how long the nearest consumer can do without. Where a place is single-buffered, load, split and sums form one ring that has to fit the period; count the ring, not only each engine's work, and don't take lists of 17.0 to 17.5 us for free in a period of 17.6. A wait that stands in front of the costly one isn't its price: here the row's 44 us on ScalarE went and periods 2 to 12 gave nothing back. And price float32 work of VectorE and GpSimd that runs at the same time, each with two inputs from SBUF, by the sum of their lone times.

## What the runs showed of the hardware that was not expected

- VectorE and GpSimd, both on float32 tiles in SBUF, took turns almost exactly: 3.34 us of lone work in 3.1 to 3.2 us (e3). VectorE's taps, whose second operand is in PSUM, kept their 1.20 us (91 taps, the longest 1.202) in periods 2 to 12 of the changed kernel too, with GpSimd busy for 168 of 226 us.
- On GpSimd a multiplication with one input of 128x512 from SBUF took 1.47 us in an inner period, more than a subtraction with two (1.27), but 2.6 us beside VectorE (e10), less than the subtraction (2.99). The pair with it went by every 2.4 us for 3.54 us of lone work: no full turn-taking.
- Removing the cause of a wait of 44 us in total on ScalarE (the row, seven waits; e1) left TensorE's time in that stretch unchanged within 3 us.
